# Block 2's front in another order: final and first norm from one chain, memory products between the projections, the first indexer and top-k steps beside the projections

## The reference

```python
    return rmsnorm(x, norm_final)            # end of block 1: x * rsqrt(mean(x*x) + eps) * g
...
        x = x + _hybrid_mixer(_rms_norm(x, norm1_g[l]), w_in[l], ...)      # block 2
        x = x + _memory_xattn(_rms_norm(x, norm2_g[l]), mem, ...)
...
    c_q, c_kv, k_idx, w_idx, q_nsa, kv_nsa, g_nsa = jnp.split(h @ w_in, splits, axis=-1)
    q_i = _rope((c_q @ w_idx_q).reshape(B, L, IDX_HEADS, IDX_DIM), pos)    # indexer queries, 8 heads
...
        idx_score = jnp.einsum('bqhs,bqh->bqs', jax.nn.relu(jnp.einsum('bqhd,bsd->bqhs', qi, k_i)), wi)
        idx_score = jnp.where(pos[None, None, :] <= t[None, :, None], idx_score, -jnp.inf)
        _, sel = lax.top_k(idx_score, k_dsa)                               # k_dsa = 128
...
    m = _rms_norm(mem, mem_norm_g)                                         # 256 memory positions
    k = _rms_norm((m @ w_xk).reshape(B, M, XATTN_HEADS, XATTN_HEAD_DIM), xk_norm_g)
    v = (m @ w_xv).reshape(B, M, XATTN_HEADS, XATTN_HEAD_DIM)
```

## Time and profile before

| | |
|---|---|
| median of 3 runs | 2751.58 us (2750.96 to 2753.2) |
| profiled execution, its own time | 2752.49 us |
| its span | 2750.7 us |
| mean granted TensorE clock | 0.946 |
| busy: PE, DVE, ACT, POOL | 2527.0, 1274.6, 1043.3, 1244.5 us |
| block 2's front, end of the last product of block 1 to the first score masked | 1794.28 to 2022.36 us |
| nsa attention | 2022.36 to 2202.30 us |

### The profile page before, as it was taken

The page is one execution under the profiler, slowest core; times in us unless marked ns, Lnnn a source line. Parts: engine busy times, 40 slices in busy tenths (PEclk is TensorE's granted clock), DMA queues, the critical chain, the costliest instruction groups (busy, mean ns, idle before and its releaser), DMA issues.

```text
span 2750.7 us, 33505 instructions
## 1 busy us (share of the span) xinstructions
PE 2527.0 (92%) x12307; PEld 2010.7 (73%) x12307; DVE 1274.6 (46%) x2501; ACT 1043.3 (38%) x1615; POOL 1244.5 (45%) x1638
## 2 busy tenths in 40 slices
PE   4999789999999999888999999988986899899998
PEld 3787567888888778666888878876744557688887
DVE  5884443353335677444343252345578754612111
ACT  4334553332222423465242232252255564433322
POOL 3533334555556634333555555562222233355553
PEclk9999899999999999899999999998888589899999
DMA  3222212332222322221232222232110001123232
GB/s 125 88 80 74 58 59 79 100 116 98 95 100 83 105 76 84 66 66 50 93 126 96 96 92 93 93 129 69 48 39 1 1 9 62 62 92 100 92 100 84
DMA packets 80291, 218.61 MB, mean 79 GB/s; under 512 B 15744, under 2 KB 25344, under 8 KB 79616
## 3 DMA queue, kind: packets, MB, share of 16 engines
q1 hardware_dynamic: 60912, 200.96, 22.5%
q10 hardware_dynamic: 19216, 15.51, 2.0%
HBM read 207.78 MB, written 2.10 MB: 76 GB/s over the span
## 4 chain that ended last, share of the span: by engine, by line
PE 78%; DVE 14%; ACT 4%; issue 2%; ACTq 1%; POOL 1%; DMA 0%; DVEq 0%
PE psG L881 23%; PE psG L882 22%; PE psG L883 22%; DVE tmp L1736 1%; PE psO L1059 1%; DVE work_m L1736 1%; PE psT L1036 1%; DVE work_b L2140 1%; PE psO L1125 1%; DVE max L2139 1%; DVE work_b L2023 1%; PE psG L1070 1%; ACTq L1410 1%; PE psS L1023 1%; DVE squares L2180 1%
## 5 line engine op out<-in xcount | busy, mean ns | idle before, releaser
L824 POOL TENSOR_TENSOR w_lo<-w_raw,w_hi 128x256 fp32r<-128x256 f32 x1494 | 1161.4, 808 | 1315.0 <-ACT w_hi L1313 1315.0
L881 PE MATMUL psG<-h_hi,w_hi 128*128 128x512 f32 x1880 | 758.8, 404 | 43.6 <-POOL w_lo L824 38.9
L882 PE MATMUL psG<-h_lo,w_hi 128*128 128x512 f32 x1880 | 743.7, 396 | 0.0
L883 PE MATMUL psG<-h_hi,w_lo 128*128 128x512 f32 x1880 | 742.9, 395 | 0.0
L1313 ACT ACTIVATE w_hi<-w_raw 128x1024 fp32r<-128x1024 f32 (+4 forms) x417 | 403.6, 969 | 486.3 <-PE psG L883 470.0
L881 PEld LDWEIGHTS psG<-h_hi,w_hi 128*128 128x128 f32 x1880 | 360.5, 192 | 131.8 <-issue 38.9
L883 PEld LDWEIGHTS psG<-h_hi,w_lo 128*128 128x128 f32 x1880 | 359.6, 191 | 77.7
L882 PEld LDWEIGHTS psG<-h_lo,w_hi 128*128 128x128 f32 x1880 | 360.0, 191 | 76.6 <-issue 3.9
L881 PE MATMUL psG<-m_hi,w_hi 128*128 128x512 f32 x800 | 312.3, 390 | 1.5 <-DVE m_lo L1736 1.5
L882 PE MATMUL psG<-m_lo,w_hi 128*128 128x512 f32 x800 | 311.7, 390 | 0.0
L883 PE MATMUL psG<-m_hi,w_lo 128*128 128x512 f32 x800 | 311.7, 390 | 0.0
(11 more groups left out here) (295 smaller groups left out, 2885.2 us busy)
## 6 DMA issues: line engine op xcount, KB each, us to landing
w_raw<-wstream SPq DMA_DIRECT2D x327, 512.0 KB, 3.3
w_raw<-wstream SPq DMA_DIRECT2D x64, 256.0 KB, 2.6
w_raw<-wstream SPq DMA_DIRECT2D x16, 384.0 KB, 3.0
work_b<-work_b ACTq DMA_DIRECT2D x16, 256.0 KB, 3.6
work_b<-cmpw ACTq DMA_DIRECT2D x2, 2048.0 KB, 8.5
x<-xT SPq DMA_DIRECT2D x4, 512.0 KB, 6.4
small_work<-ssmp ACTq DMA_DIRECT2D x8, 256.0 KB, 4.1
outT<-x SPq DMA_DIRECT2D x1, 2048.0 KB, 6.3
```

Source lines behind the costliest of these rows:

```text
L824: ins = pool.tensor_tensor(lo[:, c], w[:, c], hi[:, c].bitcast(F32), ALU.subtract)
L881: pe.matmul(out, whi, hi, start=(k == 0), stop=False)
L882: pe.matmul(out, whi, lo, start=False, stop=False)
L883: ins = pe.matmul(out, wlo, hi, start=False, stop=(k == K - 1))
```

## The change

The kernel computes the same outputs. There are three parts.

1. The first norm no longer waits for the final one. ACT squares every x tile twice, plain and times the final gain (`square_scaled`). DVE adds up both sums. Both means are taken together (`square_mean("final")`, eight small matmuls, now behind product ("xk", 0)). DVE adds (mean + eps) * eps to the scaled mean, and ACT takes the roots of both. The first norm scales x by the product of both gains (`gain2`), and the write of the final x comes after it.
2. The memory products ("xk", 3) and ("xv", 0) to ("xv", 3) move between the projections, one ahead of each of five waves (`MEMORY_AT`). `PROJECTIONS` has another order: the indexer's inputs (ki, wg, iq) come early, the compressed keys (kc) and values (vc) later. The value transposes go to `psO`.
3. From the wave of ("p2", "kc") on, two indexer or top-k steps run at the end of each wave, 18 waves and so 36 steps: all 24 of block 3, and heads 0 to 7 and four rounds of block 2. Beside units 0 to 35 of the attention there is then one step for each unit.

```diff
-PROJECTIONS = [("p2", n) for n in ("cq0", "cq1", "ckv", "kc", "ki", "wg", "ks")] + [
-    ("kvd",), ("p2", "kw"), ("kd",), ("p2", "vc"), ("iq", 0), ("p2", "vs"), ("iq", 1), ("p2", "vw"), ("iq", 2),
-    ("p2", "qn0"), ("iq", 3), ("p2", "qn1"), ("uq", 0), ("p2", "qn2"), ("uq", 1), ("p2", "qn3"), ("uq", 2), ("uq", 3)]
+PROJECTIONS = [("p2", "cq0"), ("p2", "cq1"), ("p2", "ki"), ("p2", "ckv"), ("p2", "wg"),
+               ("iq", 0), ("iq", 1), ("iq", 2), ("iq", 3), ("p2", "ks"), ("p2", "kw"), ("p2", "kc"), ("kvd",), ("p2", "vs"),
+               ("kd",), ("p2", "vw"), ("uq", 0), ("p2", "qn0"), ("uq", 1), ("p2", "vc"), ("p2", "qn1"), ("uq", 2), ("p2", "qn2"),
+               ("uq", 3), ("p2", "qn3")]
+MEMORY_AT = {("p2", "cq0"): [("xk", 0), ("xk", 1), ("xk", 2)], ("p2", "cq1"): [("xk", 3)], ("p2", "ki"): [("xv", 0)],
+             ("p2", "ckv"): [("xv", 1)], ("p2", "wg"): [("xv", 2)], ("iq", 0): [("xv", 3)]}
+MEMORY_KEYS_AT = {("p2", "ckv"): 0, ("p2", "wg"): 1, ("iq", 0): 2, ("iq", 1): 3}
+SELECT_FROM, SELECT_EACH = ("p2", "kc"), 2
...
+        tasks = [(b, r) for b in reversed(range(1, NB)) for r in range(8 + TOPK // 8)]
+        first_wave = PROJECTIONS.index(SELECT_FROM)
+        in_front = {s_: tasks[SELECT_EACH * (s_ - first_wave):SELECT_EACH * (s_ - first_wave + 1)]
+                    for s_ in range(first_wave, len(PROJECTIONS) + 4)}
+        front_tasks = sum(len(ts_) for ts_ in in_front.values())
+        def beside(i):
+
+            at = front_tasks + i
+            return tasks[at] if at < len(tasks) else None
...
+            def memory_product(key):
+
+                product(key)
+                if key == ("xk", 0):
+                    square_mean("final")
+                elif key == ("xk", 1):
+                    spread_root("norm1")
+                elif key == ("xk", 2):
+                    memory_keys_mean(0)
...
+                    if ps is block2_posts:
+                        for b, r in in_front.get(s_, []):
+                            if r < 8:
+                                indexer_head(b, r, psT[:, 0])
...
-            normalise("final", "norm_final")
-            for k in range(KD):
-                add_square("norm1", k)
-            normalise("norm1", "norm1")
+            tt(gain2[:, :], par("norm_final", 0, KD), par("norm1", 0, KD), ALU.mult)
+            dve.wait_ge(s_ms, NORMS["final"] + 1)
+            ts(root_tok[:, 0], psS[:, 0, 0:NB], eps, eps, ALU.add, ALU.mult)
+            tt(root_tok[:, 0], root_tok[:, 0], psS[:, 0, NB:2 * NB], ALU.add, s_var)
+            normalise("norm1", "norm1")
+            normalise("final", "norm_final")
```

More of the change, by code:

```diff
@@ L146, in job_plan @@
             jobs += [(("fo", l, c, i), nt, SEQ, "dve") for i in range(KD)]
-    jobs += [(("xk", i), 8, MEM, "act") for i in range(XHEADS)]
-    jobs += [(("xv", i), 8, MEM, "act") for i in range(XHEADS)]
     for key in PROJECTIONS:
+        jobs += [(m, 8, MEM, "act") for m in MEMORY_AT.get(key, [])]
         K = {"kvd": 1, "kd": 1, "iq": 2, "uq": 2}.get(key[0], 8)
@@ L786, in block_program @@
                     step(new, "cmpin")
[L787 to L790 removed]
+        tasks = [(b, r) for b in reversed(range(1, NB)) for r in range(8 + TOPK // 8)]
[3 more added lines that the diff above has]
+        front_tasks = sum(len(ts_) for ts_ in in_front.values())
+        front_heads = sum(r < 8 for ts_ in in_front.values() for b, r in ts_)
+        def beside(i):
+            at = front_tasks + i
+            return tasks[at] if at < len(tasks) else None
         all_done = dict(tally)
@@ L928, in square_mean @@
                     ins = pe.matmul(psS[:, 0, b:b + 1], tmp[:, 2, b * P:(b + 1) * P], ones[:, 0:1], start=True, stop=True)
+                if name == "final":
+                    pe.wait_ge(s_sqm1, KD - 1)
+                    for b in range(NB):
+                        ins = pe.matmul(psS[:, 0, NB + b:NB + b + 1], tmp[:, 1, b * P:(b + 1) * P], ones[:, 0:1],
+                                        start=True, stop=True)
                 ins.then_inc(s_ms, 1)
@@ L1069, in indexer_head @@
                     pe.wait_ge(s_ir, n)
-                pe.matmul(psG[:, 2, 0:W], qi[hh, h // 2, b * P:(b + 1) * P], ki[hh, 0:W],
+                else:
+                    pe.wait_ge(s_p["out"], max(by_key[key]["out"] for key in (("p2", "ki"), ("iq", 3))))
+                pe.matmul(bank[:, 0:W], qi[hh, h // 2, b * P:(b + 1) * P], ki[hh, 0:W],
                           start=True, stop=True).then_inc(s_is, 1)
@@ L1263, in _ @@
             pe.wait_ge(s_p["toksb"], block2_done["toksb"])
-            attention(units2, lambda i, w: indexer_head(*beside(i, w)) if beside(i, w) and beside(i, w)[1] < 8 else None)
+            pe.wait_ge(s_ir, front_heads)
+            attention(units2, lambda i: indexer_head(*beside(i), psG[:, 2]) if beside(i) and beside(i)[1] < 8 else None)
             for i in range(KD):
@@ L1546, in project @@
             def project(ps):
-                for new, old in waves(ps):
+                for s_, (new, old) in enumerate(waves(ps)):
+                    key = new["key"] if new else None
+                    for m in MEMORY_AT.get(key, []):
+                        if m[0] == "xk":
+                            if m[1] > 1:
+                                memory_keys_take(m[1])
+                        else:
+                            memory_values_take(m[1])
+                        if m == ("xk", 2):
+                            memory_keys_root(0)
+                        elif m == ("xv", 3):
+                            act.dma_start(cmpW.rearrange("p a b -> p (a b)"), cmpw[0]).then_inc(s_cw, 16)
+                    if key in MEMORY_MEAN_AT:
+                        memory_keys_root(MEMORY_MEAN_AT[key])
+                    if key in MEMORY_TURN_AT:
+                        memory_values_copy(MEMORY_TURN_AT[key])
                     if new:
@@ L2248, in project @@
                         windows(new)
+                    if ps is block2_posts:
+                        for b, r in in_front.get(s_, []):
+                            indexer_step(b, r)
             dve.wait_ge(s_par, 16)
```

157 lines of the change are left out of this document (79 added, 78 removed).

## The result

The changed kernel takes 2720.9 us as a median of four runs (2716.3 to 2725.8), the kernel before 2752.4 as a median of four (2751.0 to 2763.2). That is 31.5 us less, 1.1%, where 49 were predicted. The ratio on record is 0.9874, interval 0.9856 to 0.9893; it isn't the ratio of the two medians, which is 0.9886 and lies inside the interval. The profiled executions lie 36.2 us apart (2716.25 and 2752.49). The total lies in the predicted range. Its two terms do not, and they missed in opposite directions.

A forecast was written before the change was run, and what follows sets the result against it. PE was taken to set the front's pace mostly and DVE to bound the attention. Gains of 11 us in the front and 38 in the attention, 49 off 2752.5, gave 2703.5, 2703 as a median; range 2680 to 2729.

The forecast's parts named there:

- First norm and memory products: Start of the front: xk0 fills PE's wait for the norm and cq0 starts earlier; PE gains 14 us.
- Projections, wave by wave: Front's projections with the moved steps: first attention mask at 2011 instead of 2022.4 us, so the front gains 11 us.
- My own sign of being wrong: End of the front: the forecast counts as wrong if the first mask comes later than 2022 us.
- The heads: Indexer heads moved to the front: 0.43 us of matmuls each for 16, some 6 us of PE waits with kw's rotation.
- The half clock: Front's products at half clock behind PE's new waits: 3 us added.
- The rule of the Trainium skill on DVE and GpSimd: Front: two-input DVE and GpSimd exclude each other; 15 moved head additions, 0.4 us each, 6 us more, outside the sum.
- Steps moved out of the attention: Nsa attention: 42.2 us of steps leave DVE, with waits for relus; 179.9 us becomes 142, a gain of 38.
- my lower bound of 128: Nsa attention if DVE stays the bound: 128 us, a gain of 52.
- a third of the time of blocks 3 and 2 be cold: Attention: PE at half clock for a third of these blocks' time, giving groups of 11.2 and 9.4 us.
- The steps only change places in the front: Rival: steps add DVE time to waves already waiting for DVE; front +5, attention -38, total 2718; chance 0.09.
- PE at half clock becomes the attention's bound: Rival: nsa clock below about 0.6, attention 166 us, total 2727; chance 0.14.
- ACT's order: Slower rival: in the front, ACT's in-order relu delays weights and PE; steps in series, total 2791; chance 0.05.

The follow-up runs named there:

- e2: Changed kernel with only the shared chain for both norms, old order of projections, all steps beside the attention; 2742.9 us, ratio 0.9957 to the kernel before.
- e1: Changed kernel without steps in the front: new order and shared norm chain kept, all 72 steps beside the attention; 2747.2 us, ratio 0.9972 to the kernel before.
- e7: Changed kernel with only block 3's eight heads in the front, in pairs from kc on, all else beside the attention; ratio 1.0008 to the kernel before.
- e10: e9 without its rounds in the front: only block 3's eight heads there, one ahead of and one behind other phases; ratio 0.9973 to the kernel before.
- e5: Changed kernel with only block 3's 24 steps in front, heads spread, 13 rounds ahead of DVE's waits for compressed matmuls; ratio 0.9837 to the kernel before.
- e9: e5 with all 16 rounds ahead of DVE's two waits for compressed matmuls, nine and seven, none in the last waves; ratio 0.9852 to the kernel before.
- e8: e1 with the four index query products spread between ks, kw, kc and kvd instead of in a row; 2755.8 us, ratio 0.9994 to the kernel before.
- e4: Changed kernel with only block 3's 24 steps in the front, one head per wave, then two rounds per wave; ratio 0.9873 to the kernel before.
- e11: e9 with the matmuls of each of the eight front heads given out twice into the same bank; ratio 0.9849 to the kernel before.
- e12: e9 with block 2's eight heads and six of its rounds in the front too, three of block 3's rounds moved; ratio 0.9847 to the kernel before.

## Why the prediction was right in the sum and wrong in its terms

**"First norm and memory products", 14 us: right, and undersized.** xk0 stands directly behind block 1, the spread at 1802.4 (predicted 1802.1), cq0 starts at 1806.4 (1805.4) and waits 2.35 + 0.33 + 0.34 us for POOL's low parts. x's write lies beside xv0 and ki, ahead of nothing that waits. e2 measures the part alone: 16.9 us of front, of which its attention gives 6.4 back at a lower clock (0.69 against 0.74); the times say 0.43%, 12 us.

**"Projections, wave by wave", front -11: this step failed.** The whole front came out at +27.5, rounded: -16.9 (e2), +12.5 for the order (e1), +32.0 for the steps. My own sign of being wrong, a first mask later than 2022, came true (2047.6). Two of the sums were wrong.

- *The heads.* I priced a head as DVE work and as 0.43 us of PE, and waits of "some 6 us": 13 us of PE for sixteen. No row shows 0.43 us. The trace of the kernel before has the right price, 10.4 us for block 3's eight heads beside the attention:

```profile
L1070 PE MATMUL psG<-work_m 64*128 64x512 f32 x16 | 10.4, 736 | 0.6 <-ACT work_b L1472 0.6
```

  In the front a head is 1.12 us at full clock, 2.07 at half, in pairs with a wait in between: 32.4 us of PE for sixteen, as much as the 32.0 that all the steps add. I had watched DVE's free time; the in-order price was on PE. e7 shows it (18.5 us for eight), and e10 that another placement more than halves it.
- *The half clock.* I allowed 3 us. The K = 8 products vs, vw, qn0, vc, qn2 and qn3 took 6.9, 7.9, 6.6, 6.0, 7.7 and 8.3 us instead of 5.44, some 11 us in all. This came with the order and not with the steps: in e1, without steps, the same six took 43.1 us, here 43.4. The compressed keys ended at 1927.2, not 1918; kd's mean came at 1950.6, not 1930. I also took DVE to be full from there to the first mask; it was busy 68.3 of those 97 us.

Where I was right: PE waited at ki's and iq's rotations (4.7 + 0.2 + 0.5 us, half of the 10), and DVE's hole behind the compressed keys (13.4 us) stayed, because the steps come behind it in the wave. e5 and e9 fill it, and the rounds then cost nothing.

The rule of the Trainium skill on DVE and GpSimd (SBUF — State Buffer, "SBUF: two separate sides"), by which I had estimated 6 us more for fifteen additions (there are fourteen), doesn't show in size. The seven 512-column head additions in the front took 809 ns on average; beside the attention they took 751, 0.4 us in all. Those of 384 columns took 619 against 618. POOL was busy only 8.6 of the 50 us from 1900 to 1950, and 9.0 of the last 47.6, where these heads stand. Whether the additions would have been slower beside more POOL work isn't shown. The rows of DVE in the front:

```profile
L1787 DVE SCALAR_TENSOR_TENSOR work_b<-work_b,widx_tok 128x512 f32<-128x512 f32 x7 | 5.7, 809 | 8.0 <-ACT work_b L1521 7.9
L1787 DVE SCALAR_TENSOR_TENSOR work_b<-work_b,widx_tok 128x384 f32<-128x384 f32 x7 | 4.3, 619 | 2.3 <-ACT work_b L1521 2.1
```

**"Steps moved out of the attention", 38 us: right in kind, undersized.** The mechanism is as told: DVE's work fell by 39.7 us (predicted 42.2), and DVE still bounds: 106.9 of 124.2 us busy, and short gaps between 451 instructions. Its waits for relus over the nsa stretch fell from 16.0 to 2.1 us; I had counted 9.7, those ahead of the additions of blocks 3 and 2. That accounts for about 2 of the 4 us by which the stretch came below my lower bound of 128; the rest isn't taken apart. What failed is the sentence "a third of the time of blocks 3 and 2 be cold". PE's waits there shrank, the clock rose to 0.82, and groups of three units took 10.0, 8.2, 7.9 and 5.7 us (typical of each block) where I had 11.2, 9.4, 8.8 and 5.7.

**The rivals.** "The steps only change places in the front" was right in the front's sign, too mild (+5 against +27.5), and not by its mechanism: it is PE that the steps lengthen, not DVE. "PE at half clock becomes the attention's bound" was wrong (0.82 over the nsa stretch). "ACT's order" as the slower case was right in its place (PE's waits for relus) but not in its price: PE's weight loads waited 2.0 us in all for POOL's split weights, and no product ran at twice its time for that.

That the total fell into the range is luck. The front missed by 38.5 us (+27.5 against -11), the nsa attention by 18 the other way (-55.7 against -38), and small gains outside both took off some more. The forecast was near because two errors offset each other.

**What stays open.** Why the new order costs 12.5 us was split only into 5.7 us of PE without work and 4.6 us of slower matmuls (the windows begin at one clock time, the two fronts 2.1 us apart, which is the rest); e8 excludes the row of short products. How the price of the pairs divides between the wait and the place is open (e4, e7 and e10 give PE's part only). And neither single profiles nor the times can say which placement of e5, e9, e11 and e12 is best: their intervals overlap.

## What to carry to other kernels

Before work of one engine is moved into another's free time, follow each moved step through every engine that issues a part of it: here the rounds (DVE alone) were free and the heads (PE, ACT, DVE in turn) cost 2.3 us each in pairs and 1.1 us spread over earlier waves. Take each engine's price from a row of the trace where it already does the work. Put what needs no other engine just ahead of the longest wait of its own engine, and take pairs that pass through one buffer apart, one ahead of and one behind other work: here that removed the 3.3 us that PE waited between them. A wait on PE costs its own length and can cost again through the clock of what follows it: in e9 the rotation, the head and the product vs behind the wait of 2.98 us took 11.0 us, in e11, behind 1.41 us and without counting the head's second matmul, 8.0. Sum a front's waits together with the work behind them. And when two kernels are compared from a landmark, look whether the same work stands ahead of it in both.

## What was not expected of the hardware

- In one pair of profiles extra matmuls on PE cost 3.4 us where they take 8.1: they stood in a wait, and what followed ran at full clock (e11). The times of the two kernels lie some 7 us apart.
- One kernel's runs fall into groups by the granted clock: e9 has four at 2703.8 to 2708.6 us with mean clocks of 0.959 to 0.961, and two at 2726.0 and 2726.6 with 0.948. The same group of three units took 12.2 us at 0.86 and 17.4 at 0.60 in two kernels whose attention is the same (e1, e2), and 10 us of the cross part stood at 0.51 in one profile and at 1.00 in the other. Four profiles of this attention span 9 us, so smaller differences between two of them say little.
- A product of 64 rows by 512 columns that the program gives as one f32 matmul is two records and 1.12 us at full clock. A projection's 128-row matmul of split operands is 0.39 us long in its record and spaced at 0.23 us.
